# Turning the rows for the expert gather from the split operand, and splitting the first expert weights in the output projection

## The reference

```python
def rmsnorm(x, g):
    y = x * lax.rsqrt(jnp.mean(x * x, axis=-1, keepdims=True) + EPS)
    return y * g

x = x + mixer_block(h, ...)                      # ends with merged @ w_out
h = rmsnorm(x, norm_ffn[1])
logits = h @ w_router
top_v, top_i = lax.top_k(logits, 2)
top_w = softmax(top_v)
for e in range(8):
    out = out + combine[..., e:e + 1] * swiglu(h, w_gate[e], w_up[e], w_down[e])
x = x + out                                      # then the final rmsnorm
```

## Time and profile before

| | |
|---|---|
| median of three runs | 1675.69 us (1669.14 to 1677.18) |
| the profiled execution: time | 1671.14 us |
| its span | 1669.4 us |
| TensorE products busy | 95% of the span |
| VectorE, ScalarE, GpSimd busy | 61%, 51%, 15% |
| granted TensorE clock, mean | 0.98 |
| dense part ends, router begins | 1061.4 us |
| first expert product starts | 1105.5 us |

### The profile page before, as it was taken

How to read it: one execution, slowest core, us unless ns; L and a number is a source line. 1 busy time by engine, 2 the same in 40 slices (tenths; PEclk the granted TensorE clock), 3 DMA queues, 4 the chain that set the end, 5 groups by cost and what they waited for, 6 DMA issues and landing times.

```text
span 1669.4 us, 22896 instructions
## 1 busy us (share of the span) xinstructions
PE 1590.5 (95%) x7630; PEld 1325.5 (79%) x7631; DVE 1024.3 (61%) x1671; ACT 852.5 (51%) x1312; POOL 257.5 (15%) x304
## 2 busy tenths in 40 slices
PE   8999999999999999999999999879999999999991
PEld 5878888788888888888788887658788888888880
DVE  6546665654444433356467666646567889876665
ACT  5336664342323332233366643445557888875653
POOL 2003563000000000020046620310101110110102
PEclk9999999999999999999999999979999999999996
DMA  7331222232332333353321223356768999987674
GB/s 205 114 104 52 70 63 77 90 95 94 101 98 92 101 91 93 107 142 101 95 64 55 64 80 97 127 196 216 230 213 278 370 359 373 367 299 222 216 236 170
DMA packets 79111, 259.48 MB, mean 155 GB/s; under 512 B 12384, under 2 KB 12384, under 8 KB 78512
## 3 DMA queue, kind: packets, MB, share of 16 engines
q1 hardware_dynamic: 71056, 239.16, 43.3%
q0 software_dynamic: 7968, 19.21, 4.0%
HBM read 244.70 MB, written 9.47 MB: 152 GB/s over the span
## 4 chain that ended last, share of the span: by engine, by line
PE 87%; DVE 6%; issue 2%; ACT 2%; DMA 1%; POOL 0%; ACTq 0%; SPq 0%; POOLq 0%; DVEq 0%; PEldq 0%
PE ps L1366 18%; PE ps L1368 17%; PE ps L1367 17%; PE ps L1678 6%; PE ps L1680 6%; PE ps L1679 6%; PE ps L1676 4%; PE ps L1677 4%; PE ps L1521 2%; PE ps L1554 1%; DVE m_lo L1268 1%; PE ps L1534 1%; PE ps L1659 1%; PE ps L1553 1%; PE ps L1533 1%
## 5 line engine op out<-in xcount | busy, mean ns | idle before, releaser
L1268 DVE TENSOR_TENSOR m_lo<-m_raw,m_hi 128x1024 fp32r<-128x1024 f32 (+1 forms) x285 | 324.2, 1161 | 109.8 <-ACT m_hi L869 106.4
L869 ACT ACTIVATE m_hi<-m_raw 128x1024 fp32r<-128x1024 f32 (+1 forms) x285 | 284.0, 1010 | 166.4 <-PE ps L1677 130.9
L1366 PE MATMUL ps<-h_hi,w_hi 128*128 128x512 f32 x904 | 362.0, 400 | 5.5 <-DVE w_lo L959 2.9
L672 ACT ACTIVATE w_hi<-raw 128x1024 fp32r<-128x1024 f32 (+1 forms) x169 | 177.1, 1048 | 352.1 <-PE ps L1368 348.8
L1367 PE MATMUL ps<-h_lo,w_hi 128*128 128x512 f32 x904 | 354.7, 392 | 0.0
L1368 PE MATMUL ps<-h_hi,w_lo 128*128 128x512 f32 x904 | 354.6, 392 | 0.0
L959 DVE TENSOR_TENSOR w_lo<-raw,w_hi 128x1024 fp32r<-128x1024 f32 x137 | 165.6, 1209 | 147.5 <-ACT w_hi L672 147.3
L1368 PEld LDWEIGHTS ps<-h_hi,w_lo 128*128 128x128 f32 x904 | 170.6, 189 | 36.9
L1366 PEld LDWEIGHTS ps<-h_hi,w_hi 128*128 128x128 f32 x904 | 171.2, 189 | 33.7 <-DVE w_lo L959 4.7
L1367 PEld LDWEIGHTS ps<-h_lo,w_hi 128*128 128x128 f32 x904 | 171.4, 190 | 26.8 <-issue 0.7
L1678 PE MATMUL ps<-m_hi,xt_hi 128*128 128x512 f32 (+1 forms) x384 | 145.2, 378 | 6.5 <-DVE m_lo L1268 4.9
(11 more groups left out here) (244 smaller groups left out, 2852.0 us busy)
## 6 DMA issues: line engine op xcount, KB each, us to landing
m_raw<-moe_g SPq DMA_DIRECT2D x135, 512.0 KB, 5.1
m_raw<-moe_down SPq DMA_DIRECT2D x88, 512.0 KB, 5.0
raw<-w_in SPq DMA_DIRECT2D x68, 512.0 KB, 3.6
m_raw<-moe_g SPq DMA_DIRECT2D x64, 384.0 KB, 3.8
raw<-w_gu SPq DMA_DIRECT2D x44, 512.0 KB, 3.5
raw<-w_out SPq DMA_DIRECT2D x16, 512.0 KB, 3.5
raw<-w_down SPq DMA_DIRECT2D x16, 512.0 KB, 3.6
raw<-w_a SPq DMA_DIRECT2D x8, 512.0 KB, 3.5
```

What stands on the lines that cost most here:

```text
L672: A.activation(split_of(n, 0, cols)[0], raw[:, n % RAW, 0:cols], ACT.Copy).then_inc(hi_ready, 1)
L869: A.activation(m_hi[:, u % M_SPL, 0:cols], m_raw[:, u % M_RAW, 0:cols], ACT.Copy).then_inc(m_hi_ready, 1)
L1268: V.tensor_tensor(m_lo[:, u % M_SPL, 0:cols], m_raw[:, u % M_RAW, 0:cols], m_hi[:, u % M_SPL, 0:cols].bitcast(F32), ALU.subtract).then_inc ...
L1366: E.matmul(ps[:, bank, :], wh, hi, start=first, stop=False)
```

## The change

- The gain row and its multiply on GpSimd go. The rows for the gather are turned from `h_hi` and `h_lo`, which hold the gain already: `turn_h` does two products for each 128x128 block, with an F32R copy of the identity as the moving operand, and `rows_copy` on ScalarE scales them by `rinv` into `h_rows`.
- SP writes `h_rows` to `h_dram`, no longer GpSimd.
- `xs` is turned for `x_rows` only behind the lists, with its copies behind the exponential of the route on ScalarE.
- The mean squares come behind the router's products, the root behind the copy of the logits.
- The seven first expert loads are issued between the `w_out` loads, and five are split in the iterations 2 to 6 of the output units.
- SP's `weights` starts when both first gathers have landed.
- `keep_warm` is 6 and 12 where it was 12 and 24, and the one of 6 behind the logits goes.
- The places of some tiles in memory change.

```diff
-            sp.wait_ge(x_updated, 3 * KD)
-            sp.dma_start(g_row[:], ...).then_inc(rows_in, 16)
-            for u in range(M_RAW):
-                expert_unit(0, u)
@@ sync, in the loop over w_out
                     load(n + U_OUT + u, w_out[layer, u])
+                    if layer == DEPTH - 1 and u >= 3:
+                        if u == 3:
+                            sp.wait_ge(unit_done, n + U_OUT)
+                        for v in FIRST_LOADS[u - 3]:       # ((0, 1), (2, 3), (4,), (5,), (6,))
+                            expert_unit(0, v)
@@ sync, behind the router's load
+            for t in range(TT):
+                sp.wait_ge(rows_copied, t + 1)
+                sp.dma_start(h_dram[t * P:(t + 1) * P, :], h_rows[:, t, :]).then_inc(h_row_sent, 16)
+            for sl in range(SLOTS):
+                sp.wait_ge(xg_in[sl], 16)
             weights(0, N_SEC)
@@ gpsimd
-            pool.wait_ge(rows_in, 16)
-            for t in range(TT):
-                pool.wait_ge(x_copied, t + 1)
-                one(pool.tensor_tensor(h_rows[:, t, :], h_rows[:, t, :], g_row[:], ALU.mult))
-                pool.dma_start(h_dram[t * P:(t + 1) * P, :], h_rows[:, t, :]).then_inc(h_row_sent[t % 2], 16)
-            pool.wait_ge(unit_done, U_ROUTER + 1)
+            pool.wait_ge(rows_turned, TT)
             pool.memset(m_act[TAIL:P, 1, :], 0.0).then_inc(tail_clear, 1)
+            pool.wait_ge(zero_row_sent, 16)
+            pool.wait_ge(h_row_sent, 16 * TT)
             pool.wait_ge(lists_ready, 1)
@@ scalar
+            def rows_copy(q):
+                t = q % TT
+                A.wait_ge(rows_turned, q + 1)
+                rows = ps[:, x_bank(q):x_bank(q) + 2, :].rearrange("p b c -> p (b c)")
+                if q < TT:
+                    A.activation(h_rows[:, t, :], rows, ACT.Copy, scale=rinv[:, 3, t:t + 1]).then_inc(rows_copied, 1)
+                else:
+                    A.activation(x_rows[:, t, :], rows, ACT.Copy).then_inc(rows_copied, 1)
@@ scalar and vector, in the output units
+                    if layer == DEPTH - 1 and 2 <= u < 2 + M_SPL:
+                        expert_hi(16, u - 2)               # vector: expert_lo(0, u - 2)
@@ scalar, the route
             A.activation(logits_T, ps[:, LOGIT_BANK, :], ACT.Copy).then_inc(logits_ready, 1)
+            root(3)
             A.wait_ge(rinv_ready, 4)
-            for t in range(TT):
-                x_copy(t)
+            for q in range(TT):
+                rows_copy(q)
             A.wait_ge(gap_ready, 1)
             A.activation(r1[:, 3, :], r1[:, 2, :], ACT.Exp).then_inc(gap_exp, 1)
+            for q in range(TT, 2 * TT):
+                rows_copy(q)
-            for u in range(M_SPL):
-                expert_hi(16, u)                           # vector: expert_lo(0, u)
@@ tensor
+            def turn_h(t):
+                if t >= 2:
+                    E.wait_ge(rows_copied, t - 1)
+                for k in range(KD):
+                    out = ps[:, x_bank(t) + k // 4, (k % 4) * P:(k % 4 + 1) * P]
+                    E.matmul(out, h_hi[:, k, t * P:(t + 1) * P], ident_r[:], start=True, stop=False)
+                    mm = E.matmul(out, h_lo[:, k, t * P:(t + 1) * P], ident_r[:], start=False, stop=True)
+                mm.then_inc(rows_turned, 1)
@@ tensor, the route
             for k in range(KD):
-                if k == KD - 2:
-                    mean_square(3)
                 mm = h_part(U_ROUTER, LOGIT_BANK, k, 3)
             mm.then_inc(unit_done, 1)
-            turn_x(0)
+            mean_square(3)
             ... logits turned
-            turn_x(1)
-            keep_warm(6)
+            turn_h(0)
+            turn_h(1)
             ... ranks
-            turn_x(2)
-            turn_x(3)
-            keep_warm(12)
+            turn_h(2)
+            turn_h(3)
+            keep_warm(6)
             ... lists
             E.wait_ge(counts_ready, 1)
-            E.wait_ge(x_copied, TT)
+            for t in range(TT):
+                turn_x(t)
-            keep_warm(24)
+            keep_warm(12)
+            E.wait_ge(rows_copied, 2 * TT - 1)
             turn_rows(0, 0, 16)
             turn_rows(0, 1, 16)
```

More of the change, by code:

```diff
@@ L76, in build_kernel @@
         ident = sb("ident", [P, P])
+        ident_r = sb("ident_r", [P, P], F32R)
         ones = sb("ones", [P, P])
@@ L140, in build_kernel @@
         routed = ExitStack()
+        x_rows = sb("x_rows", [P, TT, D], F32, routed)
+        h_rows = sb("h_rows", [P, TT, D], F32, routed)
         m_raw = sb("m_raw", [P, M_RAW, UNIT], F32, routed)
@@ L143, in build_kernel @@
         m_lo = sb("m_lo", [P, M_SPL, UNIT], F32R, routed)
-        x_rows = sb("x_rows", [P, TT, D], F32, routed)
-        h_rows = sb("h_rows", [P, TT, D], F32, routed)
-        g_row = sb("g_row", [P, D], F32, routed)
+        gf_row = sb("gf_row", [P, D], F32, routed)
         rt = sb("rt", [P, 14, TT, EXPERTS], F32, routed)
@@ L167, in build_kernel @@
         expert = ExitStack()
+        y_in = sb("y_in", [P, 2, 2, D], F32, expert)
         xg = sb("xg", [P, SLOTS, D], F32, expert)
@@ L179, in build_kernel @@
         y_stage = sb("y_stage", [P, SLOTS, D], F32, expert)
[L180 removed]
         expert.close()
[L182 to L184 removed]
+        logits_T = y_stage[:, 0, 0:T]
         def y_of(t):
@@ L358, in load, with expert_unit @@
                 sp.dma_start(raw[:, n % RAW, 0:src.shape[1]], src).then_inc(raw_full[n % RAW], 16)
+            def expert_unit(e, u):
+                what, c, j, cols = UNITS[u % M_UNITS]
+                src = moe_down if what == "down" else moe_gu[c]
+                row = j if what == "down" else 4 * (what == "up") + j
+                sp.dma_start(m_raw[:, u % M_RAW, 0:cols], src[bass.ds(e, 1), row, :, :].rearrange("e p c -> p (e c)")
+                             ).then_inc(m_full[u % M_RAW], 16)
             def load_x(k):
@@ L656, in _ @@
             pool.sem_inc(moe_done, 1)
-            pool.wait_ge(rows_in, 32)
+            pool.wait_ge(rows_in, 16)
             for t in range(2):
                 pool.wait_ge(scaled, t + 1)
-                pool.tensor_tensor(x_rows[:, t, :], x_rows[:, t, :], gf_row, ALU.mult).then_inc(pool_out, 1)
+                pool.tensor_tensor(x_rows[:, t, :], x_rows[:, t, :], gf_row[:], ALU.mult).then_inc(pool_out, 1)
         @block.scalar
@@ L697, in bias_tile, with expert_hi @@
                              bias=nfar[:, layer, hh:hh + 1]).then_inc(bias_ready, 1)
[L699 to L704, removed]
+            def rows_copy(q):
[6 more added lines that the diff above has]
+                    A.activation(x_rows[:, t, :], rows, ACT.Copy).then_inc(rows_copied, 1)
+            def expert_hi(full, u):
+                A.wait_ge(m_full[u % M_RAW], full)
+                cols = UNITS[u % M_UNITS][3]
+                A.activation(m_hi[:, u % M_SPL, 0:cols], m_raw[:, u % M_RAW, 0:cols], ACT.Copy).then_inc(m_hi_ready, 1)
             def h_split_hi(i):
@@ L725, in _ @@
             warm_root()
+            A.wait_ge(basics, 3)
+            A.activation(ident_r[:], ident[:], ACT.Copy).then_inc(ident_ready, 1)
             split_hi(0)
@@ L959, in split_lo, with expert_lo @@
                 V.tensor_tensor(lo, raw[:, n % RAW, 0:cols], hi.bitcast(F32), ALU.subtract).then_inc(lo_ready, 1)
+            def expert_lo(done, u):
+                cols = UNITS[u % M_UNITS][3]
+                V.wait_ge(m_hi_ready, done + (u + 1))
+                V.tensor_tensor(m_lo[:, u % M_SPL, 0:cols], m_raw[:, u % M_RAW, 0:cols],
+                                m_hi[:, u % M_SPL, 0:cols].bitcast(F32), ALU.subtract).then_inc(m_lo_ready, 1)
             def lo_of(out, full, hi):
@@ L1158, in _ @@
                     h_split_lo((norm_i + 1) * KD + u)
+                    if layer == DEPTH - 1 and 2 <= u < 2 + M_SPL:
+                        expert_lo(0, u - 2)
                 rms(norm_i + 1)
@@ L1264, in _ @@
             link(V.tensor_tensor(r1[:, 5, :], r1[:, 4, :], r1[:, 3, :], ALU.mult))
-            def expert_lo(done, u):
-                cols = UNITS[u % M_UNITS][3]
-                V.wait_ge(m_hi_ready, done + (u + 1))
-                V.tensor_tensor(m_lo[:, u % M_SPL, 0:cols], m_raw[:, u % M_RAW, 0:cols],
-                                m_hi[:, u % M_SPL, 0:cols].bitcast(F32), ALU.subtract).then_inc(m_lo_ready, 1)
             def turned_x(done, sl):
@@ L1275, in turned_x @@
                     lo_of(lo, used_columns(ps[:, hb, :].rearrange("p (k c) -> p k c", c=P), sl), hi).then_inc(xt_lo_ready, 1)
-            for u in range(M_SPL):
-                expert_lo(0, u)
             turned_x(0, 0)
@@ L1339, in _ @@
                 passes(N_SEC, MORE_SEC, True)
-            V.wait_ge(rows_in, 32)
+            V.wait_ge(rows_in, 16)
             for t in range(TT + 1):
```

37 lines of the change are left out of this document (12 added, 25 removed).

## The result

| | before | after |
|---|---|---|
| median of four runs each, one chip | 1673.18 us (1669.14 to 1677.18) | 1653.35 us (1652.54 to 1654.68) |
| ratio, with its 95% interval | | 0.9887 (0.9863 to 0.9910) |
| profiled execution: time, span | 1671.14, 1669.4 us | 1653.05, 1651.3 us |
| router's first product to first expert product | 1061.38 to 1105.52: 44.14 us | 1060.99 to 1089.15: 28.16 us |

The kernel is faster by 19.8 us in the medians and by 18.1 us in the profiled spans. The last line of the table, which I call the stretch from here on, has most of it.

The account below looks back on a forecast made before the run. It took the bound to be the turn from dense work to routed experts, with TensorE waiting. First product -16.0 and 13 products -2.7 sum to -18.7; 1675.69 became 1657.0 us, own range 1652 to 1660, 8 in 10 1650 to 1664.

Parts of the forecast that it names:

- Out units: Output units before the router: five early splits and seven early loads hidden by TensorE; cost 0, bound +1 us.
- Picks: VectorE's routing: without GpSimd's multiply two stretched steps fall to 0.19, 4.75 us off; picks start at 1071.2.
- Turning: `turn_h` on TensorE: 16 products a tile at 0.112 us, 1.8 us a tile; last scaled copy ends at 1077.1.
- (3): Rival in `turn_h`: 0.23 us a product, +7.6, so -11.1 in all, 1664.6 us; chance 5%.
- (4): Rival in `turn_h`: weight load and product don't overlap, 0.61 us a product, +13.3 in all, 1689.0 us; chance 2%.
- Writing, listing, gather: Before the experts: last write lands 1079.9, lists 1078.8, gather issued 1080.8, taking 4.5 us instead of 8.60.
- rival (2): First gather stays at 8.6 us by its own cost, clock falls too: -10.4, 1665.3 us; chance 7%.
- Clock held: TensorE idles under 1 us before the first expert products; clock stays 1.00, 13 products take 3.0 not 5.7: -2.7.
- Rival (1): TensorE's clock falls among the transposes before the experts: -14.5 in all, 1661.2 us; chance 15%.
- First products: Gather landing to first expert product: 4.2 us instead of 5.6, product at 1089.5 against 1105.52, -16.0.
- From there all eight expert passes and the tail are the same: Behind the first 13 expert products: nothing more changes until the end, so the -18.7 us stays.

Follow-up runs that it names:

- late_split: Changed kernel with the five first splits of `m_raw` put back behind the route on ScalarE and VectorE, loads still early: 1658.69 us, ratio 0.9916.
- no_mult: Kernel before without GpSimd's multiply by the gain row, so the gathered rows lack the gain: 1661.59 us, ratio 0.9927.
- pool_mult: Changed kernel with two 128x1024 multiplies put back on GpSimd beside the route, on other data, nobody waiting for them: 1663.98 us, ratio 0.9952.
- pool_memset: Changed kernel with six 128x1024 memsets on GpSimd beside the route, into a place nobody reads: 1651.51 us, ratio 0.9872.
- no_hold: Changed kernel without SP's wait for the first two gathers before the stream of expert weights: 1659.76 us, ratio 0.9928.
- before_hold: Kernel before with only SP's wait for both first gathers added ahead of the expert weights: 1668.41 us, ratio 0.9974.
- turn_idle: Changed kernel with 24 more transposes in place of the twelve warming products before the turns of `xg`: 1653.80 us, ratio 0.9912.
- no_warm: Changed kernel without the twelve warming products behind the turns of `xs`: 1656.27 us, ratio 0.9923.
- pool_writes: Changed kernel with the four writes of `h_rows` issued on GpSimd's queue again: 1654.41 us, ratio 0.9910.
- ms_inside: Changed kernel with the mean squares put back among the router's products: 1656.68 us, ratio 0.9909.
- turn_8: Changed kernel turning each tile by eight transposes of `xs` instead of sixteen products; gathered rows lack the gain: 1653.19 us, ratio 0.9883.
- again: The changed kernel run again unchanged, beside the kernel before: 1653.82 us, ratio 0.9906.

## Why the prediction was right

It said 1657.0 us and -18.7; measured are 1653.35 and -19.8 in the medians and -18.1 in the spans. Of the 3.65 us between 1657.0 and 1653.35, 2.5 are the starting value: the median of the kernel before was 1675.69 in three runs and 1673.18 in four. Its steps can be laid beside the trace one by one. The router began 0.39 us sooner after, so I add 0.39 to the positions of after:

| step | forecast | measured + 0.39 |
|---|---|---|
| first routing step of VectorE | 1068.5 | 1068.49 |
| `picks` | 1071.2 | 1071.19 |
| two tiles of `turn_h` end | 1071.9 | 1071.75 |
| VectorE goes on | 1072.4 | 1072.37 |
| ScalarE's last scaled copy ends | 1077.1 | 1077.06 |
| lists | 1078.8 | 1078.39 |
| last write lands | 1079.9 | 1079.67 |
| gather issued | 1080.8 | 1080.50 |
| first slot's turns begin | 1085.3 | 1084.90 |
| first expert product | 1089.5 | 1089.54 |

**Out units: right.** Cost 0 with a bound of 1; TensorE stayed busy and the router began no later. `late_split` shows what was bought: 4.0 us in the new sequence.

**Picks: right, and the mechanism shown.** I removed 4.75 us for two stretched steps, on nothing but their coincidence with the multiplies. `no_mult` takes off 4.74, `pool_mult` brings such steps back (3.96 us) and `pool_memset` doesn't. Two details of my reading were off. The steps were not stretched exactly while a multiply ran: L1219 began at 1073.92, 0.41 us ahead of the recorded start of the second multiply (1074.33), and no run explains these 0.41. And there was a fourth such step, off the chain of waits, beside the multiply of 1084.79; it has a single input and takes 0.17 us after (VectorE, before):

```profile
1085.64 1.55 DVE L1262 TENSOR_SCALAR r<-r 128x4 f32<-128x4 f32 x1 [0.15 <-DVE lists L1258]
```

**Turning: right.** The products of `turn_h` are 0.11 us apart, as the row that I took. Rivals (3) and (4) fall with that: TensorE loads new weights for each product and overlaps the load.

**Writing, listing, gather: right.** SP's write took 2.60 us (forecast 2.8), the first gather 4.4 (4.5). `no_hold` and `before_hold` show that most of what the 8.6 us had over 4.4 came from the loads beside it, so rival (2) is excluded in both kernels; 0.8 us of it was GpSimd's longer issue, a part of its own after all.

**Clock held: right, with less room than I thought.** Rival (1) had TensorE's transposes fail to hold the clock. It did not happen, and `turn_idle` shows 6.8 us of transposes alone at 1.00. The Trainium skill (TensorE: Matmul & The Clock Gate, Part 4: PE-mode transpose) has it that transposes don't count as work for the clock; in this run the trace disagrees, and the measurement decides. But there is luck in it: `no_warm`, `pool_writes` and `ms_inside` all had about 0.50 at the first expert products. TensorE's waits ahead of the turns of the two slots were 2.91 and 1.37 us in `no_warm` and 1.01 and 1.25 in `pool_writes`, but 0.42 and 1.28 in `ms_inside`, no longer in sum than the 0.25 and 1.47 of the changed kernel. What decided it there, no run tells.

**First products: right but for one wait, and the total by cancelling.** I put 4.2 us between landing and first product and named only turns and copies. It took 4.64 (1084.51 to 1089.15). What I left out is the second slot: its gather landed 5.54 us behind its issue, 2.5 us behind the first, and TensorE waited 1.47 us for it. That wait isn't worth 1.47 us, since the turns behind it need the first `xt_lo` as well. `pool_mult` shows the path without it: both slots had landed before their turns there, TensorE waited 1.14 us for `xt_lo` instead, and the first product came 4.37 us behind the first turn, at a clock of 1.00. So the late slot costs some 0.3 us, and turns and copies alone are what I had put at 4.2. The first slot came 0.4 us sooner than forecast and the rest took 0.4 longer; that the first product lies within 0.1 us of its forecast is luck. A version that gathers the 64 rows first or splits the slots otherwise was not tried.

**Not forecast: what follows.** The 13 products at full clock brought 84.03 - 81.29 = 2.74 us (forecast 2.7), which is the first section, from its first product to its output copy, before and after. The second section gave 1.44 back at the border, and from there to the end 0.4 was gained. With the head start of 0.39 and the 15.98 of the stretch, the sum is -0.39 - 15.98 - 2.74 + 1.44 - 0.4 = -18.1. "From there all eight expert passes and the tail are the same" is the one sentence of the forecast that failed, by 1.44 us.

How the parts share the 16 us of the stretch: the multiply alone is 9.6, the hold alone 3.4. The remaining 3.0 is what no run took apart in the old sequence: the reordering, with all that was measured above at 0.5 to 1.3 us apiece, and the turns of `xg` at full clock. The parts don't simply add up: the hold is worth 3.4 us in the old sequence and 5.1 in the new, and the early split 4.0 in the new (in the old it was not run). No version that ran beats the changed kernel by more than the runs scatter: `pool_memset` (1651.51) and `turn_8` (1653.19) have ratios whose intervals overlap with those of the changed kernel.

## What to carry to other kernels

When a short operation of VectorE takes ten times its usual length, look at what GpSimd reads at that moment, in a timeline of both; moving the GpSimd work away can be worth more than the time it takes itself. When one transfer sets the end of a stage, hold the transfers that nobody needs yet behind it, and move the work that its old length covered (here five splits) to a place with spare engine time, or the gain is taken back. Price each wait of TensorE twice: by its own length, and by the products behind it at half pace.

## What the runs showed of the hardware

- VectorE's steps with both inputs in SBUF were held by GpSimd's multiply, which reads SBUF, to its end (2.34 and 2.00 us for a step of 0.19 in `pool_mult`), and not by memsets, which only write (`pool_memset`, 6.01 us of them). A reduction inside a multiply of `pool_mult` kept its 0.19; a TENSOR_SCALAR with one input beside a multiply of the kernel before did not (1.55 us, 0.17 after). For two inputs the Trainium skill (SBUF — State Buffer, Who interferes with whom) says the same: such a VectorE instruction contends with a GpSimd instruction that reads SBUF, not with one that only writes it.
- A gather of 512 KB shows 4.4 us alone (1.04 of it GpSimd's issue), 8.0 to 8.6 us with weight loads of the same size issued over 2 us ahead of it, and 6.0 us with one issued 0.86 us ahead; two writes of 512 KB started 1.1 us apart show 3.84 us for the second, against 2.60 for one that starts 1.8 us behind the one before it (the changed kernel).
- A clock that has fallen can stay down while TensorE is busy throughout: 15 us at 0.50 in `pool_mult`, from 1075.3 to 1090.9, although in the kernel before it came back behind 16 transposes (from 1077.42 to 1080.66). In `pool_mult` TensorE ran the rank products, those of `turn_h`, six warming products and the list products from 1075.3 on, then 32 transposes from 1086.72, and the clock rose inside these. In the changed kernel the same products of `turn_h` kept a clock of 1.00. I have no explanation.
- The border of the first two expert sections has the same wait of 2.8 to 2.9 us in TensorE in the kernel before and in the changed one (2.1 to 3.0 in all runs). `again` ran to see whether the dip behind it is chance; it has the same one. All six profiled kernels whose first expert products ran at full clock show a dip there (mean clock 0.83 in the 10 us from 1 us ahead of the first product behind the wait: the changed kernel, `again`, `turn_idle`, `turn_8`, `pool_memset` and `pool_mult`). Of the eight at half clock there six show none (the kernel before, `before_hold`, `no_hold`, `late_split`, `pool_writes`, `ms_inside`), two do (`no_warm`, `no_mult`, 0.83 as well). So part of what a held clock brings at the first products was given back at this border, in every run that held it. Whether the same wait falls into a dip seems to hang on its moment; no run tells what decides it, and it stays open.
